# A 31-tap depthwise convolution: tap blocks made on chip, and four taps moved from TensorE to ScalarE and GpSimd

## The chip, the cores and the metric

The kernel runs on one core of a Trainium2 chip. The metric is device time in microseconds (us) of one execution. Before the change three runs gave 1594.94, 1595.30 and 1595.79 us, with a median of 1595.3 us.

## The reference

One inference step of a two-layer encoder trunk, for 256 frames of a new stream and 16 frames each of 8 running streams: 384 tokens of 1024 features, all in fp32. Layer 1 has a SwiGLU feed-forward block, a Conformer convolution module and a second feed-forward block. Layer 2 has the same with attention in the middle. The convolution module is what is changed:

```python
def _conv_module(h, prev, pw1_w, pw1_b, dw_w, dw_b, cln_g, cln_b, pw2_w, pw2_b):
    u = h @ pw1_w + pw1_b
    u = u[..., :D_MODEL] * jax.nn.sigmoid(u[..., D_MODEL:])
    u_full = jnp.concatenate([prev, u], axis=1)          # prev: the 30 rows before
    z = lax.conv_general_dilated(u_full, dw_w[:, None, :], window_strides=(1,),
        padding='VALID', feature_group_count=D_MODEL) + dw_b   # 31 taps, each channel alone
    z = jax.nn.silu(_layer_norm(z, cln_g, cln_b))
    return z @ pw2_w + pw2_b, u_full[:, -(CONV_K - 1):]
```

So each output of the depthwise convolution is a sum of 31 products of a channel's value at 31 neighbouring frames with 31 weights of that channel.

## The kernel before, in words

Activations lie with the features on the 128 partitions: 8 tiles (`KT`) of 128 features by 384 tokens, 256 of them (part 0) of the new stream, 128 (part 1) of the eight running ones. A dense product is made of units: a 128x1024 block of weights lands in `raw`, ScalarE rounds it to fp32r in `wH` (line 788), VectorE takes the rest into `wL` (line 1047), and TensorE makes three 384-column products for each 128x128 block (lines 1494 and 1502). The ring holds four units: unit n+4 is refilled when TensorE is through with unit n, and each refill has its fixed place in ScalarE's and VectorE's programs. Every engine has one instruction stream written out by hand, which it runs in order; they meet at semaphores. There is no scheduler.

The convolution stage runs over the tiles d = 0 to 7. For tile d, TensorE makes the two pointwise products (units 2d and 2d+1 of the stage, banks 2j and 2j+1 with j = d % 2). ScalarE takes the sigmoid of the second (line 897), VectorE multiplies and writes the gated row `uF[:, d]` (lines 1340 and 1341). SP and ScalarE then issue 16 DMAs, eight each (`shifted_rows`, line 402), which copy the 128 rows of `uF[:, d]` into four tiles `u4`, shifted by 0 to 3 frames in the four groups of 32 partitions. With these, one TensorE product of a 128x32 block does four taps for 32 channels: the block holds a diagonal of weights for each tap. `taps(d)` on TensorE (line 1671) goes over 7 groups (`QUADS`) of four taps, 4 groups of channels and the two parts, 56 matmuls, and comes three tiles late: `taps(d-3)` stands after the pointwise products of tile d, and `taps(5)`, `taps(6)`, `taps(7)` follow the last of them. The blocks with the diagonals (128x896 for a tile) are made on the host and loaded by DMA (line 412). The three taps that are left are done by VectorE on `uF` (`rest_taps`, lines 1317 to 1322), which starts from the subtracted mean `cS` for tiles 1 to 7, and `conv_out_tile` (line 1330) adds them to TensorE's bank, into `z[:, d]`.

`cS` is the mean of tile 0 of `z`: VectorE makes `z[:, 0]` in its round for tile 3, TensorE multiplies it by ones between the two units of tile 4 (`shift`, line 1572), and ScalarE copies the result (line 797) at the head of its round for tile 4. GpSimd has little to do in the stage: the residual `xa` (lines 694 and 696), the subtraction from tile 0 (line 633), the 16 copies of the last 30 frames for the output (lines 723 and 724), and the running sums of the tiles and of their squares (`zs`, line 646, and `sqs`, line 655) up to tile 6. The squares come from ScalarE (line 809). Two last products with ones (lines 1576 to 1587) give mean and variance for the layer norm, which ends the stage.

ScalarE's round for tile d before the change:

```python
            for d in range(KT):
                refill(n + RING, 2 * j)              # the first unit of tile d + 2
                a.activation(sg[:, j, :], ...)       # sigmoid of tile d
                refill(n + RING + 1, 2 * j + 1)      # the second unit of tile d + 2
                shifted_rows(act, d, 2)              # 8 DMA issues, which wait for u_done
                shifted_rows(act, d, 3)
                if d > 3:
                    square(1, d - 4)
```

Of the kernel before, what the change touches and what calls it, by code (L numbers as in the profile page):

```python
# [21 lines left out]
P = 128  # L22
# [13 lines left out]
QUADS = CK // 4  # L36
REST = CK - 4 * QUADS
# [59 lines left out]
_par("dw_rest", REST * KT)  # L97
# [48 lines left out]
def build_program(nc, W, ADA0, ADA, par_d, con_d, x_d, c_d, conv_d, cw_d, kt_d, v_d, lf_d, wf_d,  # L146
                  y_o, kT_o, v_o, lf_o, conv_o, nc_d):
    with ExitStack() as ctx:
# [31 lines left out]
        taps4 = at("taps4", [P, 2, QUADS + 1, P], hid + 4 * KT * UW)  # L180
        o4 = hid + 4 * KT * UW + 8 * (QUADS + 1) * P
# [5 lines left out]
        assert o4 + 56 * UW <= hid + 2 * FT * T * 4  # L187
# [72 lines left out]
        tapsT = at("tapsT", [P, QUADS, P], tmp.manual_sbuf_range[0])  # L260
# [48 lines left out]
        taps_in = [sem(f"taps_in{i}") for i in range(3)]  # L309
        u4_in = [sem(f"u4_in{i}") for i in range(4)]  # L310
        silu_done, rest_done = sem("silu_done"), sem("rest_done")
# [15 lines left out]
        TAP_PLACE = ((0, 0), (1, 0), (0, 1), (1, 1), (0, 2), (2, 0), (0, 3), (1, 2))  # L327
# [77 lines left out]
        def tap_tile(d):  # L405

            s = TAP_PLACE[d][0]
            return tapsT[:] if s == 2 else taps4[:, s, 0:QUADS]

        def load_taps(queue, d):  # L410

            queue.dma_start(tap_tile(d), cw_d[d].rearrange("p (q c) -> p q c", q=QUADS))\
                .then_inc(taps_in[TAP_PLACE[d][0]], 16)

# [4 lines left out]
        def _(sp):  # L419
# [99 lines left out]
            load_taps(sp, 1)  # L519
            load_taps(sp, KT - 3)  # L520
# [17 lines left out]
            sp.wait_ge(cv_mm, KT - 2)  # L538
            piece(B_CONV_GAP[2], 0)
# [85 lines left out]
        def _(pool):  # L625
# [87 lines left out]
            residual(1)  # L713
            center(1, 0)
            for k in range(1, KT - 1):
                add_tile(1, k)
                add_square(1, k)
                if k == 4:
                    pool.wait_ge(u_done, 2 + KT)
                    pool.wait_ge(cv_mm, k + 1)  # L720
                    for d in range(KT):
                        to = conv_st[:, d] if d < KT - 1 else conv_end[:]
                        g.tensor_copy(to[:, 0:HIST], uF[:, d, SEQ:SEQ + HIST])
                        op = g.tensor_copy(
                            to[:, HIST:].rearrange("p (b t) -> p b t", b=DB),
                            uF[:, d, HIST + SEQ:UROW].rearrange("p (b t) -> p b t", b=DB)[:, :, DS:DS + HIST])
                    op.then_inc(convst_ok, 1)
# [52 lines left out]
        def _(act):  # L780
# [108 lines left out]

            for d in range(KT):  # L890
                j, n = d % 2, U_PW1 + 2 * d
                if d == 4:
                    shift(1)
                refill(n + RING, 2 * j)
                act.wait_ge(w_used, n + 2)
                act.wait_ge(u_done, d + 1)
                a.activation(sg[:, j, :], bank[2 * j + 1][:, 0:T], ACT.Sigmoid,
                             bias=pcol("pw1_b", KT + d)).then_inc(sig_done, 1)
                refill(n + RING + 1, 2 * j + 1)
                act.wait_ge(u_done, 2 + d + 1)  # L900
                if d > 3:
                    act.wait_ge(cv_mm, d - 3)
                shifted_rows(act, d, 2)
                if d == KT - 1:
                    act.wait_ge(cv_mm, KT - 3)
                    load_taps(act, KT - 2)
# [127 lines left out]
        def _(dve):  # L1034
# [267 lines left out]

            def rest_taps(d):
# [3 lines left out]
                shift = (cS[:, 0:SEQ], cS[:, SEQ:T].rearrange("p (b t) -> p b t", b=DB))  # L1307
                if d > 0:
                    dve.wait_ge(cs_done, 2)
                if d > 1:  # L1310
                    dve.wait_ge(z_ready, 2 + KT + d - 1)
                for q in range(REST):
                    w = pcol("dw_rest", KT * q + d)
                    for part in range(2):
                        src = window(uF[:, d], 4 * QUADS + q)[part]
                        if q == 0 and d == 0:
                            op = v.tensor_scalar(acc[part], src, w, None, ALU.mult)
                        elif q == 0:
                            op = v.scalar_tensor_tensor(acc[part], src, w, shift[part], ALU.mult, ALU.subtract)
# [13 lines left out]
            for d in range(KT):  # L1333
# [12 lines left out]
                if d > 2:  # L1346
                    conv_out_tile(d - 3)
            rest_taps(KT - 3)
            conv_out_tile(KT - 3)
            rest_taps(KT - 2)  # L1350
# [130 lines left out]
        def _(pe):  # L1481
# [174 lines left out]
            def taps(d):  # L1656

                out = bank[4 + d % 2]
                place, use = TAP_PLACE[d]
                weights = tap_tile(d)  # L1660
                pe.wait_ge(taps_in[place], 16 * use + 16)
# [258 lines left out]
def _tap_blocks(w):  # L1920
# [3 lines left out]
    cw = np.zeros((KT, 4, 32, QUADS, 4, 32), np.float32)  # L1924
    c = np.arange(32)
    cw[:, :, c, :, :, c] = taps.reshape(QUADS, 4, KT, 4, 32).transpose(4, 2, 1, 0, 3)
    return cw.reshape(KT, P, QUADS * P)
# [81 lines left out]
```

## Time and profile before

| | us |
|---|---|
| median of three runs | 1595.3 |
| the profiled execution | 1594.26 |
| its span | 1592.5 |
| PE busy in the span | 1559.2 (98%) |
| DVE busy | 796.0 (50%) |
| ACT busy | 594.4 (37%) |
| POOL busy | 263.7 (17%) |
| the convolution stage, from its first separate unit to the last product with ones | 345.93 to about 441 |

In the chain of waits, "issue" is time in which an engine waited for nothing that the profile shows. An engine name with a q, as ACTq, is its queue of DMA issues.

### The profile page before, as it was taken

The page shows a single profiled execution, that of the slowest core. Times are in us where ns is not written, and L with a number is a line of the kernel's source. Part 1 is how long each engine was busy: PE and PEld are TensorE (multiplying, and loading weights), DVE is VectorE, ACT ScalarE, POOL GpSimd, SP SyncE. Part 2 cuts the span into 40 slices and gives each one's busy share as a digit, 9 for nine tenths or more (in the row PEclk, how much of TensorE's full clock was granted, in tenths as well). Part 3 has the DMA queues.
Part 4 walks back from the last instruction along what each step waited for, and adds up shares of the span by engine and source line. Part 5 has one row for each costly group of instructions (what it writes and reads, how often), then busy time and mean ns, then how long its engine had stood idle before and what let it go on. Part 6 is the DMA issues. An engine that isn't in the chain of part 4 may idle for free.

```text
span 1592.5 us, 31097 instructions
## 1 busy us (share of the span) xinstructions
PE 1559.2 (98%) x12550; PEld 1493.5 (94%) x12550; DVE 796.0 (50%) x1246; ACT 594.4 (37%) x897; POOL 263.7 (17%) x307
## 2 busy tenths in 40 slices
PE   6999999999999999999999999999998999999998
PEld 5999999998789999999988999999997899999997
DVE  3433344475588434344654433344567684444443
ACT  3433333342155333333343433333346554333332
POOL 1100002250335000012340000002252052000111
PEclk9999999999999999999999999999999999999999
DMA  9545466579983455556417554566556824333441
GB/s 373 182 163 184 158 216 222 183 238 276 275 336 102 172 195 179 191 199 225 163 54 252 188 183 158 182 226 236 187 220 242 290 94 132 132 121 118 143 142 44
DMA packets 86748, 301.66 MB, mean 189 GB/s; under 512 B 10784, under 2 KB 14160, under 8 KB 85328
## 3 DMA queue, kind: packets, MB, share of 16 engines
q1 hardware_dynamic: 83440, 294.55, 54.1%
q10 hardware_dynamic: 3216, 5.80, 1.4%
q8 instruction: 68, 1.11, 0.3%
q14 instruction: 24, 0.20, 0.0%
HBM read 283.31 MB, written 6.32 MB: 182 GB/s over the span
## 4 chain that ended last, share of the span: by engine, by line
PE 87%; DVE 5%; issue 3%; ACT 2%; DMA 1%; POOL 1%; SPq 1%; ACTq 0%; DVEq 0%; POOLq 0%
PE bank L1494 71%; PE bank L1502 8%; PE bank L1531 3%; DVE wL L1047 1%; PE bank L1731 1%; DMA land<-ADA 1%; ACT wH L788 1%; PE bank L1671 1%; PE bank L1825 1%; PE bank L1796 1%; DVE hL L1185 1%; DVE z L1082 0%; PE bank L1767 0%; SPq L495 0%; DVE z L1089 0%
## 5 line engine op out<-in xcount | busy, mean ns | idle before, releaser
L788 ACT ACTIVATE wH<-raw 128x1024 fp32r<-128x1024 f32 x328 | 345.6, 1057 | 507.3 <-PE bank L1494 469.9
L1494 PE MATMUL bank<-hH,wH 128*128 128x384 f32 x1496 | 502.9, 336 | 0.8 <-DVE wL L1047 0.8
L1047 DVE TENSOR_TENSOR wL<-raw,wH 128x1024 fp32r<-128x1024 f32 x328 | 415.8, 1294 | 174.3 <-ACT wH L788 171.4
L1494 PE MATMUL bank<-hH,wL 128*128 128x384 f32 x1496 | 500.0, 334 | 0.0
L1494 PE MATMUL bank<-hL,wH 128*128 128x384 f32 x1496 | 499.8, 334 | 0.0
L1494 PEld LDWEIGHTS bank<-hH,wH 128*128 128x128 f32 x1496 | 280.8, 188 | 5.1 <-DVE wL L1047 2.4
L1494 PEld LDWEIGHTS bank<-hL,wH 128*128 128x128 f32 x1496 | 280.9, 188 | 0.4
L1494 PEld LDWEIGHTS bank<-hH,wL 128*128 128x128 f32 x1496 | 280.8, 188 | 0.0
L1230 DVE TENSOR_TENSOR tmp<-sg,bank 128x384 f32<-128x384 f32 x88 | 48.8, 554 | 431.8 <-PE bank L1494 414.2
L1494 PE MATMUL bank<-hidH,wH 128*128 128x384 f32 x704 | 237.0, 337 | 0.0
L1494 PE MATMUL bank<-hidH,wL 128*128 128x384 f32 x704 | 235.3, 334 | 0.0
L1494 PE MATMUL bank<-hidL,wH 128*128 128x384 f32 x704 | 235.2, 334 | 0.0
L633 POOL TENSOR_TENSOR z<-z,cS 128x384 f32<-128x384 f32 x7 | 8.1, 1162 | 890.0 <-ACT cS L797 890.0
L854 ACT ACTIVATE sg<-bank 128x384 f32<-128x384 f32 x88 | 43.2, 491 | 254.5 <-PE bank L1494 235.6
L1494 PEld LDWEIGHTS bank<-hidH,wH 128*128 128x128 f32 x704 | 132.2, 188 | 1.7 <-DVE z L1219 0.6
L1494 PEld LDWEIGHTS bank<-hidL,wH 128*128 128x128 f32 x704 | 132.2, 188 | 0.5
L1494 PEld LDWEIGHTS bank<-hidH,wL 128*128 128x128 f32 x704 | 132.2, 188 | 0.0
L1502 PE MATMUL bank<-hH,wH 128*128 128x384 f32 x232 | 79.4, 342 | 4.4 <-DVE hL L1185 2.6
L1502 PE MATMUL bank<-hH,wL 128*128 128x384 f32 x232 | 77.7, 335 | 0.0
L1502 PE MATMUL bank<-hL,wH 128*128 128x384 f32 x232 | 77.6, 335 | 0.1
L655 POOL TENSOR_TENSOR sqs<-sqs,sqb 128x384 f32<-128x384 f32 x34 | 50.8, 1495 | 147.5 <-ACT sqb L809 147.5
L809 ACT ACTIVATE sqb<-z 128x384 f32<-128x384 f32 x56 | 28.6, 516 | 65.1 <-DVE z L1219 26.3
(224 smaller groups left out, 1578.1 us busy)
## 6 DMA issues: line engine op xcount, KB each, us to landing
raw<-W SPq DMA_DIRECT2D x328, 512.0 KB, 3.7
araw<-ADA SPq DMA_DIRECT2D x52, 512.0 KB, 5.7
gapZ<-ADA SPq DMA_DIRECT2D x36, 512.0 KB, 4.9
land<-ADA SPq DMA_DIRECT2D x16, 512.0 KB, 15.3
gapE<-ADA SPq DMA_DIRECT2D x16, 512.0 KB, 4.2
KTb<-kt_d SPq DMA_DIRECT2D x8, 1024.0 KB, 7.0
Vb<-v_d SPq DMA_DIRECT2D x8, 1024.0 KB, 5.2
gapH<-ADA SPq DMA_DIRECT2D x12, 512.0 KB, 4.5
```

The lines of the kernel that those rows point to most:

```text
L655: g.tensor_tensor(sqs[:], sqs[:], sqb[:, k % 2], ALU.add).then_inc(sqs_done, 1)
L788: a.activation(wH[:, slot, :], raw[:, slot, :], ACT.Copy).then_inc(w_hi, 1)
L809: a.activation(sqb[:, k % 2], z[:, k, :], ACT.Square).then_inc(sq_done, 1)
L854: a.activation(sg[:, j, :], bank[2 * j][:, 0:T], ACT.Silu).then_inc(sg_done, 1)
L1047: v.tensor_tensor(wL[:, slot, :], raw[:, slot, :], wH[:, slot, :].bitcast(F32), ALU.subtract)\
L1185: v.tensor_tensor(lo[:, ks, :], src[:, ks, :], hi[:, ks, :].bitcast(F32), ALU.subtract)\
L1230: v.tensor_tensor(tmp[:, j, :], sg[:, j, :], bank[2 * j + 1][:, 0:T], ALU.mult)\
L1494: op = mm(out, tile_w(w, slot, k), m[:, k0 + k, :], start=start and k == 0 and q == 0, stop=stop and k == nk - 1 and q == 2)
L1502: op = mm(bank[j][:, 0:T], tile_w(w, j, k), m[:, k, :], start=k == 0 and q == 0, stop=k == KT - 1 and q == 2)
L1531: op = mm(out[32 * j:32 * j + 32, 0:cols], cact[:, k, :], tile[:, cols * j:cols * j + cols], start=start, stop=stop)
L1671: op = mm(acc, weights[:, q, rows], src, start=q == 0, stop=q == QUADS - 1)
L1731: op = mm(bank[4 * half + t][:, :], h[:, k, tok], w[:, j, 512 * kk:512 * kk + 512], start=k == 0 and q == 0, stop=k == KT - 1 and q == 2)
```

## The change

- TensorE does 6 groups of four taps and not 7: 48 matmuls for a tile and not 56.
- The four taps 24 to 27 (`INNER`) go to ScalarE and GpSimd. ScalarE multiplies the windows of `uF[:, d]` by a column of weights: the first product goes to `z[:, d]`, the next three into the two halves of `tmp` in turn, each in two parts. GpSimd adds these three to `z[:, d]`. For tiles 1 to 7 GpSimd then subtracts `cS` from it. ScalarE's products for tile d stand at the end of its round for tile d. Before the first one it waits for the residual `xa`, which reads the old `z`.
- VectorE's three taps (28 to 30) now start from `z[:, d]`; they wait for `taps_moved` (for tile 0 for `pool_taps`) where before they waited for `cS`.
- The blocks with the diagonals aren't loaded any more. One small load brings the weights and a 32x32 identity for all tiles (128x224), and VectorE multiplies them out to 128x768 for each tile (`make_taps`).
- GpSimd's order is other: its copies of the last frames now stand behind the three sums of tile 7.

```diff
-QUADS = CK // 4
-REST = CK - 4 * QUADS
+QUADS = 6
+INNER = 4
+REST = CK - 4 * QUADS - INNER
...
-                if 2 < d < KT - 1:
-                    sp.wait_ge(cv_mm, d - 2)
-                    load_taps(sp, d - 1 if d < KT - 2 else KT - 1)
-
-            load_taps(sp, 0)
-            load_taps(sp, 1)
-            load_taps(sp, KT - 3)
+
+            sp.dma_start(tapw[:], cw_d).then_inc(taps_in, 16)
...
             sp.wait_ge(cv_mm, KT - 2)
+            sp.wait_ge(pool_taps, (INNER - 1) * KT)
             piece(B_CONV_GAP[2], 0)
...
+            def add_taps(d):
+
+                for q in range(1, INNER):
+                    pool.wait_ge(act_taps, INNER * d + q + 1)
+                    if q > 1:
+                        pool.wait_ge(pool_taps, (INNER - 1) * d + q - 1)
+                    g.tensor_tensor(z[:, d, :], z[:, d, :], tmp[:, (q - 1) % 2, :], ALU.add).then_inc(pool_taps, 1)
+
+            def shift_taps(d):
+
+                pool.wait_ge(cs_done, 2)
+                pool.wait_ge(pool_taps, (INNER - 1) * (d + 1))
+                g.tensor_tensor(z[:, d, :], z[:, d, :], cS[:], ALU.subtract).then_inc(taps_moved, 1)
+
+            for d in range(4):
+                add_taps(d)
+            for d in range(1, 4):
+                shift_taps(d)
             center(1, 0)
-            for k in range(1, KT - 1):
+            for d in range(4, KT):
+                add_taps(d)
+                shift_taps(d)
+                if d == KT - 1:
+                    pool.wait_ge(cv_mm, 5)
+                    for t in range(KT):
...
+                add_tile(1, d - 3)
+                add_square(1, d - 3)
+            for k in range(5, KT - 1):
                 add_tile(1, k)
                 add_square(1, k)
...
+            def inner_taps(d):
+
+                if d == 0:
+                    act.wait_ge(xa_done, 2 * KT)
+                for q in range(INNER):
+                    if d > 0 and q in (1, 2):
+                        act.wait_ge(pool_taps, (INNER - 1) * d + 1 - q)
+                    elif q == 3:
+                        act.wait_ge(pool_taps, (INNER - 1) * d + 1)
+                    to = z[:, d] if q == 0 else tmp[:, (q - 1) % 2]
+                    parts = (to[:, 0:SEQ], to[:, SEQ:T].rearrange("p (b t) -> p b t", b=DB))
+                    for part in range(2):
+                        op = a.activation(parts[part], window(uF[:, d], 4 * QUADS + q)[part], ACT.Identity,
+                                          scale=pcol("dw_rest", KT * q + d))
+                    op.then_inc(act_taps, 1)
...
                 shifted_rows(act, d, 3)
                 if d > 3:
                     square(1, d - 4)
+                inner_taps(d)
...
+            def make_taps(d):
+
+                if d < 2:
+                    dve.wait_ge(taps_in, 16)
+                else:
+                    dve.wait_ge(cv_mm, d - 1)
+                n = 4 * QUADS
+                v.tensor_tensor(taps4[:, d % 2, 0:QUADS * P].rearrange("p (n c) -> p n c", n=n),
+                                tapw[:, n * d:n * d + n].unsqueeze(2).to_broadcast([P, n, 32]),
+                                tapw[:, n * KT:n * KT + 32].unsqueeze(1).to_broadcast([P, n, 32]), ALU.mult)\
+                    .then_inc(taps_made, 1)
+
+            make_taps(0)
+            make_taps(1)
...
                 if d > 0:
-                    dve.wait_ge(cs_done, 2)
+                    dve.wait_ge(taps_moved, d)
+                else:
+                    dve.wait_ge(pool_taps, INNER - 1)
...
                     conv_out_tile(d - 3)
+                    make_taps(d - 1)
...
-                pe.wait_ge(taps_in[place], 16 * use + 16)
+                pe.wait_ge(taps_made, d + 1)
```

ScalarE before, its round for tile 1: `wH` is a refill, `sg` the sigmoid, the DMA rows are the shifted copies.

```order
L788 ACTIVATE wH<-raw 128x1024 [waits w_in2,w_used]
L897 ACTIVATE sg<-bank,par 128x384 [waits u_done,w_used]
L788 ACTIVATE wH<-raw 128x1024 [waits w_in3,w_used]
L402 DMA u_64<-uF 32x652 [waits u_done]
L402 DMA u_64<-uF 32x652 x7
```

And after, the same round:

```order
L802 ACTIVATE wH<-raw 128x1024 [waits w_in2,w_used]
L927 ACTIVATE sg<-bank,par 128x384 [waits u_done,w_used]
L802 ACTIVATE wH<-raw 128x1024 [waits w_in3,w_used]
L403 DMA u_64<-uF 32x652 [waits u_done]
L403 DMA u_64<-uF 32x652 x7
L916 ACTIVATE z<-uF,par 128x256
L916 ACTIVATE z<-uF,par 128x128
L916 ACTIVATE tmp<-uF,par 128x256 [waits pool_taps]
L916 ACTIVATE tmp<-uF,par 128x128
```

Behind these stand two more such pairs into `tmp`, and then the refill of the next round. So eight activations now stand between the shifted copies of one tile and the refills of the next.

GpSimd before, from the sums of tile 4 to the end of the stage (14 more copies stand where the dots are); `zs` is the running sum of tiles, `sqs` that of squares, `conv_st` the output copies.

```order
L723 COPY conv_st<-uF 128x30 [waits cv_mm,u_done]
L724 COPY conv_st<-uF 128x240
...
L646 TENSOR_TENSOR zs<-zs,z 128x384 [waits ys_done,z_ready]
L655 TENSOR_TENSOR sqs<-sqs,sqb 128x384 [waits sqs_done,sq_done]
L646 TENSOR_TENSOR zs<-zs,z 128x384 [waits ys_done,z_ready]
L655 TENSOR_TENSOR sqs<-sqs,sqb 128x384 [waits sqs_done,sq_done]
L633 TENSOR_TENSOR z<-z,cS 128x384 [waits cs_done]
```

And after, from the sums of tile 7's products:

```order
L712 TENSOR_TENSOR z<-z,tmp 128x384 [waits act_taps]
L712 TENSOR_TENSOR z<-z,tmp 128x384 [waits pool_taps,act_taps] x2
L718 TENSOR_TENSOR z<-z,cS 128x384 [waits pool_taps,cs_done]
L732 COPY conv_st<-uF 128x30 [waits cv_mm]
L733 COPY conv_st<-uF 128x240
...
L637 TENSOR_TENSOR zs<-zs,z 128x384 [waits ys_done,z_ready]
L646 TENSOR_TENSOR sqs<-sqs,sqb 128x384 [waits sqs_done,sq_done]
```

The last two rows come three times, for tiles 4, 5 and 6. The copies and three pairs of sums now stand behind the last product of tile 7; before, the copies and two pairs stood behind the fifth round of taps and nothing of tile 7.

VectorE after, its round for tile 4 (`mS` is the accumulator of tile 1, `uF` the gated row of tile 4):

```order
L1362 SCALAR_TENSOR_TENSOR mS<-uF,par,z 128x256 [waits taps_moved]
L1362 SCALAR_TENSOR_TENSOR mS<-uF,par,z 128x128
...
L1383 SCALAR_TENSOR_TENSOR uF<-bank,par,sg 128x256 [waits sig_done]
L1384 SCALAR_TENSOR_TENSOR uF<-bank,par,sg 128x8x16
```

Before:

```order
L1319 SCALAR_TENSOR_TENSOR mS<-uF,par,cS 128x256 [waits cs_done]
L1319 SCALAR_TENSOR_TENSOR mS<-uF,par,cS 128x128
...
L1340 SCALAR_TENSOR_TENSOR uF<-bank,par,sg 128x256 [waits sig_done]
L1341 SCALAR_TENSOR_TENSOR uF<-bank,par,sg 128x8x16
```

The head of the round now waits for GpSimd's `taps_moved`, behind four tiles of ScalarE's products, where it waited for the copy of the mean.

## Rows read from the trace of the kernel before

**Rows 1.** Windows of the stage: length, busy time of each engine, PE clock, DMA.

```profile
383.00:419.00 36.00, 36.00 (x417) 32.11 (x419) 13.36 (x29) 8.69 (x12) 3.96 (x4) 1.00 0.97 274
```

**Rows 2.** TensorE in order of time: start, length, idle time before in brackets.

```profile
345.93 0.41 PE L1494 MATMUL bank<-hH,wH 128*128 128x384 f32 x1 [0.82 <-DVE wL L1047]
...
362.75 4.76 PE L1671 MATMUL bank<-u,taps 128*32 128x256 f32 x112
...
371.71 0.81 PE L1572 MATMUL bank<-z,con 128*128 128x384 f32 x2
```

**Rows 3.** ScalarE in order of time, rounds 1 to 5.

```profile
350.09 1.06 ACT L788 ACTIVATE wH<-raw 128x1024 fp32r<-128x1024 f32 x1 [5.50 <-issue]
351.05 0.56 ACT L897 ACTIVATE sg<-bank,par 128x384 f32<-128x384 f32 x1
351.52 1.05 ACT L788 ACTIVATE wH<-raw 128x1024 fp32r<-128x1024 f32 x1
352.43 5.04 ACTq L402 DMA_DIRECT2D u<-uF  x8
...
359.91 6.04 ACTq L402 DMA_DIRECT2D u<-uF  x8
...
374.90 0.49 ACT L797 ACTIVATE cS<-bank 128x384 f32<-128x384 f32 x1 [6.06 <-issue]
...
378.94 6.51 ACTq L402 DMA_DIRECT2D u<-uF  x8
385.50 0.53 ACT L809 ACTIVATE sqb<-z 128x384 f32<-128x384 f32 x1 [7.26 <-issue]
...
392.19 5.60 ACTq L402 DMA_DIRECT2D u<-uF  x8
```

**Rows 4.** ScalarE's groups over the whole span, shapes apart: busy, mean ns.

```profile
L836 ACT ACTIVATE h<-z,Bm,Am 128x256 f32<-128x256 f32 x40 | 23.4, 592 | 28.8 <-DVE Bm L1161 13.8 <-DMA z<-x_d 10.7 <-DVE z L1089 4.3
L841 ACT ACTIVATE hH<-h 128x384 fp32r<-128x384 f32 x34 | 17.9, 526 | 22.9 <-POOL h L685 22.3 <-DVE h L1148 0.2
L920 ACT ACTIVATE h<-z,par 128x384 f32<-128x384 f32 x8 | 5.7, 708 | 2.9 <-DVE z L1089 2.0 <-PE bank L1531 0.3
L883 ACT ACTIVATE conR<-con 128x128 fp32r<-128x128 f32 x1 | 0.3, 292 | 0.0
```

**Rows 5.** GpSimd in order of time.

```profile
352.52 2.46 POOL L696 TENSOR_SCALAR xa<-z,gA,bA 128x128 f32<-128x128 f32 x1
375.47 1.32 POOL L633 TENSOR_TENSOR z<-z,cS 128x384 f32<-128x384 f32 x1 [20.50 <-ACT cS L797]
...
429.52 0.27 POOL L723 COPY conv_st<-uF 128x30 f32<-128x30 f32 x1
...
434.36 1.18 POOL L646 TENSOR_TENSOR zs<-zs,z 128x384 f32<-128x384 f32 x1
...
437.65 1.04 POOL L655 TENSOR_TENSOR sqs<-sqs,sqb 128x384 f32<-128x384 f32 x1
```

**Rows 6.** GpSimd's two groups over the whole span: busy, mean ns.

```profile
L646 POOL TENSOR_TENSOR zs<-zs,z 128x384 f32<-128x384 f32 x27 | 35.8, 1328 | 36.4 <-DVE z L1219 36.4
L633 POOL TENSOR_TENSOR z<-z,cS 128x384 f32<-128x384 f32 x7 | 8.1, 1162 | 890.0 <-ACT cS L797 890.0
```

**Rows 7.** VectorE in order of time.

```profile
344.42 2.51 DVE L1047 TENSOR_TENSOR wL<-raw,wH 128x1024 fp32r<-128x1024 f32 x2
...
382.84 0.74 DVE L1319 SCALAR_TENSOR_TENSOR rstd<-uF,par,cS 128x256 f32<-128x256 f32 x2
383.50 1.40 DVE L1322 SCALAR_TENSOR_TENSOR rstd<-uF,par,rstd 128x256 f32<-128x256 f32 x4
391.41 0.48 DVE L1340 SCALAR_TENSOR_TENSOR uF<-bank,par,sg 128x256 f32<-128x256 f32 x1 [6.52 <-ACT sg L897]
```

**Rows 8.** Windows at the start and end of the span, columns as in Rows 1.

```profile
0.00:10.00 10.00, 1.93 (x64) 1.72 (x64) 0.45 (x4) 1.70 (x2) 0.20 (x4) 1.00 0.83 291
1584.00:1592.00 8.00, 3.65 (x12) 1.84 (x10) 4.29 (x9) 5.05 (x8) 0.00 (x0) 0.92 0.50 197
```

More of the change, by code:

```diff
@@ L308, in build_program @@
             "hist_ok", "sig_done", "u_done", "cv_mm", "convst_ok"))
-        taps_in = [sem(f"taps_in{i}") for i in range(3)]
+        taps_in, taps_made = sem("taps_in"), sem("taps_made")
         u4_in = [sem(f"u4_in{i}") for i in range(4)]
-        silu_done, rest_done = sem("silu_done"), sem("rest_done")
+        silu_done, rest_done, act_taps, pool_taps, taps_moved = (sem(n) for n in (
+            "silu_done", "rest_done", "act_taps", "pool_taps", "taps_moved"))
         kf_done, vs_done, f_mm, lf_chain, ncum_done, lfo_done = (sem(n) for n in (
@@ L405, in tap_tile @@
         def tap_tile(d):
[L407 to L413, printed above, removed]
+            return taps4[:, d % 2, 0:QUADS * P].rearrange("p (q c) -> p q c", q=QUADS)
         block = ctx.enter_context(nc.Block())
@@ L713, in _ @@
             residual(1)
-            center(1, 0)
-            for k in range(1, KT - 1):
+            def add_taps(d):
[12 more added lines that the diff above has]
+                shift_taps(d)
+            center(1, 0)
+            for d in range(4, KT):
[4 more added lines that the diff above has]
+                    for t in range(KT):
+                        to = conv_st[:, t] if t < KT - 1 else conv_end[:]
+                        g.tensor_copy(to[:, 0:HIST], uF[:, t, SEQ:SEQ + HIST])
+                        op = g.tensor_copy(
+                            to[:, HIST:].rearrange("p (b t) -> p b t", b=DB),
+                            uF[:, t, HIST + SEQ:UROW].rearrange("p (b t) -> p b t", b=DB)[:, :, DS:DS + HIST])
+                    op.then_inc(convst_ok, 1)
+                add_tile(1, d - 3)
+                add_square(1, d - 3)
+            for k in range(5, KT - 1):
                 add_tile(1, k)
                 add_square(1, k)
[L718 to L727, printed above, removed]
             sums(2)
@@ L1312, in rest_taps @@
                 for q in range(REST):
-                    w = pcol("dw_rest", KT * q + d)
+                    w = pcol("dw_rest", KT * (INNER + q) + d)
                     for part in range(2):
[L1315 to L1319, printed above, removed]
+                        src = window(uF[:, d], 4 * QUADS + INNER + q)[part]
+                        if q == 0:
+                            op = v.scalar_tensor_tensor(acc[part], src, w, inner[part], ALU.mult, ALU.add)
                         else:
@@ L1923, in _tap_blocks @@
     taps[:] = w[:4 * QUADS]
[L1924 to L1927, printed above, removed]
+    of = taps.reshape(QUADS, 4, KT, 4, 32).transpose(1, 4, 2, 0, 3).reshape(P, KT * 4 * QUADS)
+    return np.concatenate([of, np.tile(np.eye(32, dtype=np.float32), (4, 1))], 1)
 def _constants():
@@ L1963 @@
     put("dw_b", _cols(i["dw_b"]))
-    put("dw_rest", np.concatenate([_cols(i["dw_w"][0][4 * QUADS + q]) for q in range(REST)], 1))
+    put("dw_rest", np.concatenate([_cols(i["dw_w"][0][4 * QUADS + q]) for q in range(INNER + REST)], 1))
     par[0:H, PAR["b_f"][0]] = i["b_f"]
```

18 lines of the change are left out of this document (7 added, 11 removed).

## The prediction

> **What bounds the kernel now.** I read the busy times first: TensorE is busy for 1559.2 of 1592.5 us, so at first sight all that is taken from it is gained. Then the windows of the convolution stage: from 383 to 419 us TensorE has no gap at all, at a granted clock of 1.00, while ScalarE seems busy for 8.69 of 36 us [rows 1]. That share misleads, since DMA issues are not in it. In order of time ScalarE's refill at 350.09 had been idle 5.50 us for "issue": the eight shifted copies of tile 0 held the engine [rows 3]. A round of ScalarE is a refill, the sigmoid, a refill (starts 350.09, 351.05, 351.52, 352.43: 2.34 us together) and eight issues: 5.04, 6.04, 6.51 and 5.60 us for eight in four rounds, so 23.19/32 = 0.725 us each, 5.8 us a round [rows 3]. That is 8.1 us. A round of TensorE is two units, (362.75 - 345.93)/4 = 4.2 us each, and 4.7 us of taps from tile 3 on [rows 2]: 8.4 us at first, 13.1 us later. So ScalarE is full in the first rounds and has about 4.5 us to spare in the later ones. The stage ends in GpSimd's sums: the last one is over at 437.65 + 1.04 = 438.69 us [rows 5], and the products with ones wait for it.
>
> **What is taken away.** TensorE: one of seven groups, 4.7/7 = 0.67 us a tile, 5.4 us in all [rows 2]. SP issues fewer loads and ScalarE one less; both wait or have room there, and I count that at nothing. If nothing else came late the stage would be 5.4 us shorter at most.
>
> **VectorE's blocks.** 768 columns with two operands from SBUF. The nearest row is the 1024-column subtraction, 2.51 us for two [rows 7], so 0.95 us; by columns alone from the same row also 0.94. Two are made ahead of the first gated row, which delays the first unit by about 1.1 us (TensorE already waits 0.82 there [rows 2]); this vanishes in what follows. The other six lie where VectorE idles, as the 6.52 us before 391.41 [rows 7]. I take nothing, bounds 0 and 2.
>
> **ScalarE's products.** Each tap is an activation of 256 and one of 128 columns with its scale read from a column. The 256-column one with scale and bias from columns takes 592 ns; from 256 to 384 columns that form rises to 708, so 128 columns take about 0.48 [rows 4]. Back to back each starts 0.09 us before the last has ended (the refill of 1.06 us at 350.09 and the next start at 351.05 [rows 3]). So 0.50 + 0.39 = 0.9 us a tap. The bounds: as cheap as a plain copy (292 ns at 128 columns, 526 at 384, so 0.41 at 256 [rows 4]), less the overlaps, 0.52; and 1.07 without overlap. I take 0.9, since the form with a scale column is the nearest. Four taps are 3.6 us, and the fourth must wait until GpSimd has added the second (its half of `tmp` must be free): a sum of 1.08 us (four in the 4.33 us from 434.36 to 438.69 [rows 5]) and 0.06 us to each side against the 0.9 of the third product, so 0.3 us. A tile costs ScalarE 3.9 us, eight cost 31. In the later rounds nearly all the room is used; in the first ones none is there.
>
> **The walk.** The products of tile 0 wait for the residual, over at 352.52 + 2.46 = 355.0 [rows 5]; they are done at 358.9. Only then does ScalarE refill the first unit of tile 3, which was done at 350.09 before. Sigmoid 360.4, gated row 361.1, VectorE's half of the refill 1.2 us later: TensorE starts tile 3 at 362.4 and not at 354.3, after a wait of about 7 us. Rounds 1, 2 and 3 of ScalarE are 2.34 + 5.8 + 3.9 = 12.0 us: 395.0. In between TensorE meets its second wait. The product of the mean stands between the two units of tile 4 and needs `z[:, 0]`, which VectorE makes in round 3, behind the gated row and the refills. The sigmoid of tile 3 ends at 358.9 + 24.1 + 1.4 = 384.4; gated row 0.7, refills 2.4 (half of 2.51 each, less overlap), `z` 0.6: 388.1. TensorE is there at 362.4 + 8.4 + 4.0 + 4.2 = 379.0 and waits 9 us. Before, it came to that point at 371.71 without a wait [rows 2].
>
> Round 4: the copy of the mean 0.4, refills and sigmoid 2.34: 397.7. Now the shifted copies need the gated row of tile 4, which in VectorE stands behind its three taps of tile 1, which now wait for GpSimd: third sum of tile 3 at 396.1, subtraction of the mean 1.16 (its mean time [rows 6]) 397.3, taps 0.66 + 1.40 [rows 7] 399.4, gated row 400.1. A wait of 2.4 us. Then issues, a square of 0.5 and products: 410.3. Rounds 5, 6 and 7 are 2.34 + 5.8 + 0.5 + 3.9 = 12.5 us: 447.9. GpSimd then adds the last product (449.1), subtracts the mean (450.2), makes the 16 copies, which took 434.36 - 429.52 = 4.84 us [rows 5] (455.1), and adds three tiles and three squares, six sums of 1.08 (461.6). Against 438.69 that is 22.9 us later. TensorE, from 388.1 on, comes to about 453 with its taps, inside this. What follows in the stage and behind it is as before. The profiled execution took 1594.26 us: 1594.3 + 22.9 = 1617.2; the median of runs was 1.0 us above it. I say 1617.
>
> **A rule on the sums.** GpSimd's sum of two 384-column tiles took 1.04 to 1.18 us at the stage's end [rows 5], but 1328 ns in the mean of all 27 [rows 6]. The Trainium skill (SBUF — State Buffer, "SBUF: two separate sides") says that VectorE and GpSimd share a pair of ports which one locks for a whole instruction, also against a VectorE operation with two SBUF inputs, while ScalarE has its own. The trace agrees in direction: the residual's piece at 352.52 took 2.46 us beside VectorE's 1024-column subtraction. In a sentence that the sum does not need: by this rule the new sums, which meet VectorE's refills and blocks more often, would come at 1.3 and not at 1.08.
>
> **Rivals.**
> 1. *The issues do not hold ScalarE* (the other side). If products could run beside the issues, its round would be 2.34 + 3.9 + 0.5 = 6.7 us, under TensorE's 12.4 everywhere; TensorE's 5.4 us would be gained, less 1.1 at the first unit: 1590. It decides from where ScalarE's round is under TensorE's. Against it: the refill at 350.09 that had been idle 5.50 us for the issues, when units had long been free [rows 3]. 4%.
> 2. *It is all off the path* or gain and loss are even: 1594. Nothing in the rows makes them equal. 2%.
> 3. *Cheap products and issues.* 0.52 us a tap takes 0.38 x 32 = 12 us from ScalarE's sum, and issues as in round 1 (0.63) take 56 x 0.095 = 5 us. Then TensorE's own series is next, so not all of it counts: from about 1604 to 1611, say 1608. For it: the windows are read in plain order. Against it: the scale from a column. 20%.
> 4. *GpSimd under contention.* Sums of 1.33 us [rows 6] add 0.25 us at eight waits, the last product and six sums, 3.8 us, and full-length products (1.07) 5.4: 1626. 12%.
> 5. *The clock.* In the first 10 us of the span TensorE is busy for 1.93 us and the granted clock is 1.00; in the last window, 3.65 us busy of 8, it is 0.92 [rows 8]. If it fell to 1.2 GHz after the waits of 7, 9 and 8 us, a unit would take 8.4 us for 4.2 and the two products at the end the same: up to 4 us for each wait, of which those of the middle hide behind ScalarE: 1621. 7%. The Trainium skill (TensorE: Matmul & The Clock Gate, "What's actually happening") says that an idle array is set to 1.2 GHz until work returns; by that rule this rival would be certain, and the row of the start speaks against it.
>
> **Chances and range.** The forecast, 1612 to 1622, has 55%. Adding both lower ends gives about 1604 and both upper ends with contention about 1630; 8 in 10 lie in 1605 to 1628. A measurement of this kernel tells 0.2% (3.2 us) from no change. Faster is rival 1, 4%; same is rival 2, 2%; the rest is slower, 94%.
>
> **What would show it.** In the profile after: ScalarE without idle time other than "issue" from 355 to about 448; eight activations of `uF` in 3.9 us a tile; TensorE waiting some 7 us for `wL` ahead of tile 3 and some 9 us for `z` ahead of the mean of tile 4, with its taps 4.0 us long; VectorE waiting for GpSimd at the head of round 4; the copies behind the last products, and the sums over at about 461. It is wrong if TensorE has no gap between 345 and 430, if a tap costs under 0.6 us, or if the stage ends under 450.

## The result, and the profile after

The changed kernel takes 1615.7 us in the median of four runs (1614.75 to 1620.26), the one before 1595.2 us beside it. The ratio is 1.0128, with an interval of 1.0112 to 1.0144: slower by 20.5 us. The forecast was 1617 us with a range of 1605 to 1628, so sign and size came out. The profiled execution took 1614.82 us with a span of 1612.7, against 1594.26 and 1592.5: 20.6 us more. Not all of it came the way I had put it, as the rest shows.

The busy times on the page of the changed kernel (us, share of the span, instructions of each engine):

```profile
PE 1560.4 (97%) x12422; PEld 1494.7 (93%) x12422; DVE 803.0 (50%) x1254; ACT 617.2 (38%) x961; POOL 298.8 (19%) x338
```

TensorE has fewer products and is yet busy for 1.2 us longer: a first sign that some of them ran slowly. Its waits between 335 and 475 us (what waited, for whom, sum, times, longest):

```profile
PE bank L1621 <- POOL zs L637: 9.1, 1, 9.1
PE bank L1539 <- DVE wL L1075: 7.6, 2, 5.9
PE bank L1617 <- DVE z L1373: 4.1, 1, 4.1
```

These are the three gaps that were forecast: for the refill of tile 3 (5.9 of the 7.6 us; the other 1.7 lie ahead of the first unit), for `z` ahead of the mean of tile 4, and for GpSimd's sums at the end. TensorE in order of time, to set beside [rows 2]:

```profile
347.03 0.41 PE L1539 MATMUL bank<-hH,wH 128*128 128x384 f32 x1 [1.70 <-DVE wL L1075]
...
361.50 0.66 PE L1539 MATMUL bank<-hH,wH 128*128 128x384 f32 x1 [5.91 <-DVE wL L1075]
361.96 0.52 PE L1539 MATMUL bank<-hL,wH 128*128 128x384 f32 x1
362.28 0.52 PE L1539 MATMUL bank<-hH,wL 128*128 128x384 f32 x1
...
371.96 0.33 PE L1539 MATMUL bank<-hL,wH 128*128 128x384 f32 x1
372.13 0.34 PE L1539 MATMUL bank<-hH,wL 128*128 128x384 f32 x1
...
384.96 1.65 PE L1617 MATMUL bank<-z,con 128*128 128x384 f32 x2 [4.07 <-DVE z L1373]
```

After the wait of 5.91 us the products follow each other every 0.32 us; ten us later every 0.17. The same product costs about twice as much right behind a wait. The windows say why (columns as in [rows 1]):

```profile
363.00:371.00 8.00, 8.00 (x38) 8.00 (x37) 0.71 (x3) 5.17 (x11) 3.03 (x3) 0.77 0.96 259
379.00:388.00 9.00, 4.93 (x18) 4.01 (x18) 4.40 (x6) 3.88 (x8) 2.09 (x3) 0.77 0.65 197
400.00:420.00 20.00, 20.00 (x224) 18.10 (x226) 10.54 (x21) 10.14 (x23) 7.54 (x8) 1.00 0.92 283
...
455.00:465.00 10.00, 8.01 (x104) 5.10 (x108) 3.17 (x8) 3.88 (x5) 2.80 (x3) 0.63 0.80 322
```

The granted clock is a mean between two levels, 2.4 and 1.2 GHz. It is 1.00 where TensorE had no gap (400 to 420), 0.77 around the two waits in the middle and 0.63 behind the 9.1 us at the end. This fits what the Trainium skill (TensorE: Matmul & The Clock Gate, "What's actually happening") says of an idle array, whose clock is let down to 1.2 GHz. The start of the span [rows 8], by which I gave that rule 7 in 100, was no evidence against it, as two rows of the kernel before show:

```profile
7.85 1.93 PE L1531 MATMUL bank<-land,cact 128*32 128x64 f32 x64 [7.85 <-DMA land<-ADA]
...
23.51 2.23 PE L1531 MATMUL bank<-land,cact 128*32 128x64 f32 x128
```

Records of the same kind of product took 1.93/64 = 0.030 us each in the first ten us and 2.23/128 = 0.017 at 23.5 us, though the granted clock reads 1.00 in both stretches. So a reading of 1.00 at the start does not show fast products. That the clock was low there is likely, but no record shows it.

ScalarE in order of time, beside [rows 3]:

```profile
354.62 0.80 ACT L916 ACTIVATE z<-uF,par 128x256 f32<-128x256 f32 x2 [9.80 <-POOL xa L687]
355.33 1.48 ACT L916 ACTIVATE tmp<-uF,par 128x256 f32<-128x256 f32 x4
357.23 0.81 ACT L916 ACTIVATE tmp<-uF,par 128x256 f32<-128x256 f32 x2 [0.42 <-POOL z L712]
357.94 1.04 ACT L802 ACTIVATE wH<-raw 128x1024 fp32r<-128x1024 f32 x1
...
360.25 5.11 ACTq L403 DMA_DIRECT2D u<-uF  x8
...
421.29 5.91 ACTq L403 DMA_DIRECT2D u<-uF  x8
```

A tap starts 0.71 us after the one before it (354.62, 355.33), and a tile's four, with the wait of 0.42 us for GpSimd's sum, take 357.94 - 354.62 = 3.32 us, not 3.9. The two shapes apart (busy, mean ns of one):

```profile
L916 ACT ACTIVATE tmp<-uF,par 128x256 f32<-128x256 f32 x24 | 12.0, 499 | 3.7 <-POOL z L712 3.7
L916 ACT ACTIVATE tmp<-uF,par 128x128 f32<-128x128 f32 x24 | 9.4, 393 | 0.0
```

VectorE in order of time, beside [rows 7]:

```profile
384.29 0.61 DVE L1373 SCALAR_TENSOR_TENSOR z<-bank,par,rstd 128x384 f32<-128x384 f32 x1
384.82 0.94 DVE L1338 TENSOR_TENSOR taps<-tapw 128x768 f32<-128x768 f32 x1
393.19 2.24 DVE L1362 SCALAR_TENSOR_TENSOR mS<-uF,par,z 128x256 f32<-128x256 f32 x2 [7.42 <-POOL z L718]
395.35 2.15 DVE L1365 SCALAR_TENSOR_TENSOR mS<-uF,par,mS 128x256 f32<-128x256 f32 x4
397.41 0.47 DVE L1383 SCALAR_TENSOR_TENSOR uF<-bank,par,sg 128x256 f32<-128x256 f32 x1
```

A block takes 0.94 us alone, as worked out. The head of round 4 waits for GpSimd, and the gated row of tile 4 comes at 397.4 to 398.15. GpSimd's end of the stage, beside [rows 5]:

```profile
442.02 3.87 POOL L712 TENSOR_TENSOR z<-z,tmp 128x384 f32<-128x384 f32 x3 [0.38 <-ACT tmp L916]
446.04 1.27 POOL L718 TENSOR_TENSOR z<-z,cS 128x384 f32<-128x384 f32 x1
447.26 0.27 POOL L732 COPY conv_st<-uF 128x30 f32<-128x30 f32 x1
...
452.05 0.98 POOL L637 TENSOR_TENSOR zs<-zs,z 128x384 f32<-128x384 f32 x1
...
456.80 1.00 POOL L646 TENSOR_TENSOR sqs<-sqs,sqb 128x384 f32<-128x384 f32 x1
```

The last sum is over at 457.80 against 438.69: 19.1 of the 20.6 us stand there. The chain that ended last goes on from it (start, us, what). The profile shows each product of these fp32 kinds as two records: the 56 of `taps(d)` before are x112 in [rows 2], so x2 is one product. First before, then after:

```profile
437.83 0.88 PE bank L1576 x2
...
440.95 2.76 PE bank L1531 x96
443.71 1.64 issue
```

```profile
393.69 3.90 PE bank L1715 x96
397.60 8.54 PE bank L1539 x48
...
456.99 1.62 PE bank L1621 x2
...
461.17 1.28 PE bank L1632 x2
462.44 5.38 PE bank L1576 x192
467.82 12.22 PE bank L1547 x69
```

The same four products (eight records) took 3.1 us before and 5.45 after, 2.3 us more; they are at 1.2 GHz behind the wait. The next piece then gives back 1.85 us: its 192 records were held up for 1.64 us in the middle before, and now run through in 5.38. So the next piece's end is at 467.82 against 448.18, 19.6 us later, and little more is added up to the span's end (20.2).

### The profile page after: what moved, and what is told of

Its sections match the earlier page's. It is cut to its first block, busy times and chain, and to the rows that moved or that the text cites. A ratio compares the mean times of both kernels' runs of the same rounds, so it can differ in the third digit from the quotient of the medians.

```text
span 1612.7 us, 30960 instructions
## 1 busy us (share of the span) xinstructions
PE 1560.4 (97%) x12422; PEld 1494.7 (93%) x12422; DVE 803.0 (50%) x1254; ACT 617.2 (38%) x961; POOL 298.8 (19%) x338
## 4 chain that ended last, share of the span: by engine, by line
PE 88%; DVE 4%; ACT 2%; POOL 2%; issue 1%; DMA 1%; ACTq 1%; SPq 1%; DVEq 0%; POOLq 0%
PE bank L1539 71%; PE bank L1547 7%; PE bank L1576 4%; DMA land<-ADA 1%; PE bank L1775 1%; ACTq L403 1%; ACT wH L802 1%; PE bank L1715 1%; DVE wL L1075 1%; DVE hL L1213 1%; PE bank L1869 1%; PE bank L1840 1%; DVE z L1117 0%; POOL xa L685 0%; DVE z L1110 0%
## 5 line engine op out<-in xcount | busy, mean ns | idle before, releaser
L1539 PEld LDWEIGHTS bank<-hH,wH 128*128 128x128 f32 x1496 | 282.3, 189 | 12.3 <-issue 9.3
```

Of the source, the lines that this page charges most:

```text
L1539: op = mm(out, tile_w(w, slot, k), m[:, k0 + k, :], start=start and k == 0 and q == 0, stop=stop and k == nk - 1 and q == 2)
```

## The experiments

All are compared with the kernel before on the same chip, and their edits are shown against the changed kernel where nothing else is said.

**Without the products and their sums.** ScalarE's products and GpSimd's sums go, VectorE begins from `cS` as before, and GpSimd's copies and sums stand again as in the kernel before; the blocks and the six groups stay. Taps 24 to 27 are then missing from the result.

```diff
-            for d in range(4):
-                add_taps(d)
-            for d in range(1, 4):
-                shift_taps(d)
...
-                inner_taps(d)
...
-                    dve.wait_ge(taps_moved, d)
-                else:
-                    dve.wait_ge(pool_taps, INNER - 1)
+                    dve.wait_ge(cs_done, 2)
```

> The changed kernel without ScalarE's products and GpSimd's sums: taps 24 to 27 are left out of the result, TensorE does six groups, VectorE makes the blocks and does its three taps as before. Theory A (the products hold ScalarE and with it the refills, the gated rows and the last sums; the rest of the change is worth what TensorE saves): TensorE starts the stage about 1.1 us late behind the two blocks, then saves 0.67 us in each of 8 tiles, so about 4 us faster than before: 1591, from 1589.5 to 1592.5, and no wait of TensorE over 2 us between 347 and 430 us. Rival B (the blocks on VectorE delay the gated rows or the taps): 1596 or more, with TensorE waiting for the blocks.

Measured: ratio 0.9997 (0.9988 to 1.0006), no change, where I had expected 1591. Two things follow. The whole loss comes with the products, the sums and the order of GpSimd's work. And TensorE's saving is worth nothing by itself. TensorE's longest wait in that run:

```profile
PE bank L1581 <- POOL zs L636: 5.1, 1, 5.1
```

The 5.4 us that six groups save lie there as a wait of 5.1 us for GpSimd's sums, which end at 438.23 + 1.00 = 439.23, half a us later than before. Behind that wait the four products with ones took 4.33 us (438.42 to 442.75) in place of 3.12: slow products take 1.2 us of the saving. TensorE was almost without a gap before and still not alone in setting the end.

**The blocks alone.** All seven groups on TensorE, their blocks made by VectorE; the computation is whole.

```diff
-QUADS = 6
-INNER = 4
+QUADS = CK // 4
+INNER = 0
```

GpSimd's order is that of the kernel before again.

> The kernel before with the blocks for seven groups made by VectorE (896 columns) in place of the loads, and nothing on ScalarE and GpSimd; nothing is left out. Theory A: the two blocks ahead of the first gated row cost about 1.2 us once, the others lie in VectorE's idle time; fewer DMA issues are worth nothing: 1596.5, from 1595.3 to 1598. Rival B: each block delays the path by its own length, about 1.1 us a tile: 1602 or more.

Measured: ratio 1.0011 (1.0002 to 1.0020), 1.8 us slower, near the upper one of my bounds, 0 and 2. Making the blocks on chip brings no time. In its profile TensorE waits 2.0 us at the first unit and 2.1 us for the sums, and the four products behind that take 4.69 us (439.72 to 444.41) in place of 3.12.

**The products without the sums.** ScalarE makes all products, nobody adds them, and GpSimd's copies and sums stand as in the kernel before. The result is again without taps 24 to 27.

```diff
-                    if d > 0 and q in (1, 2):
-                        act.wait_ge(pool_taps, (INNER - 1) * d + 1 - q)
-                    elif q == 3:
-                        act.wait_ge(pool_taps, (INNER - 1) * d + 1)
-                    to = z[:, d] if q == 0 else tmp[:, (q - 1) % 2]
+                    if 4 * d + q > 1:
+                        act.wait_ge(act_taps, 4 * d + q - 1)
+                    to = tmp[:, q % 2]
```

> The changed kernel with ScalarE's products made but not used: GpSimd does no sums of them and no subtractions, VectorE starts from the mean as before, so taps 24 to 27 are missing in the result. Theory A (ScalarE's occupancy is the loss up to the last round, GpSimd's part only its sums and their place behind the last tile): both waits of TensorE, 5.9 us ahead of tile 3 and some 4 us ahead of the mean of tile 4, stay, the end comes 4 to 7 us earlier than in the changed kernel: 1610, from 1608 to 1612. Rival B (GpSimd's sums are the loss): 1600 or less, near the kernel without products, 1595.6.

Measured: ratio 1.0094 (1.0079 to 1.0110), 15.1 us slower. TensorE's waits:

```profile
PE bank L1515 <- DVE wL L1051: 7.1, 2, 5.4
PE bank L1597 <- POOL zs L637: 5.6, 1, 5.6
PE bank L1593 <- DVE z L1349: 3.7, 1, 3.7
```

All three gaps stay. So 15 of 20 us come with ScalarE's work alone, and GpSimd's sums of products, its subtractions and their order add 5. The parts do not simply add up: GpSimd's copies lie between ScalarE's last squares and the last sums in this run too (443.70 to 448.53), so a part of the 15 us is theirs.

**Four of ScalarE's eight shifted copies issued by SP.**

```diff
-                for t in range(2):
+                for t in range(3):
...
-                shifted_rows(act, d, 2)
```

> The changed kernel with four of ScalarE's eight shifted copies of each tile issued by SP. ScalarE's round is 2.6 us shorter. Theory A (ScalarE's occupancy sets the pace up to the mean of tile 4, later ScalarE and TensorE are level): the wait ahead of tile 3 stays (it comes from the residual), the one ahead of the mean of tile 4 goes, and the last products are over 5 to 8 us earlier: 1608, from 1605 to 1611. Rival B (SP's twelve issues a tile, or the copies' landing, are late in turn): 1613 or more. Rival C (GpSimd's sums, not ScalarE, are the pace): no change, 1615 to 1616.

Measured: ratio 1.0065 (1.0049 to 1.0080) where the changed kernel has 1.0128 (1.0112 to 1.0144): 9.6 to 10 us of the loss go, and nothing of the computation was changed. ScalarE's rounds 1 and 2 take 8.1 and 8.4 us (refills at 357.81, 365.95 and 374.30), where they took 10.8 and 11.1 in the changed kernel (357.94, 368.75, 379.82). TensorE's two longest waits:

```profile
PE bank L1538 <- DVE wL L1074: 7.6, 2, 5.9
PE bank L1620 <- POOL zs L637: 5.3, 1, 5.3
```

The first gap stays: the products of tile 0 wait for the residual, whoever issues. The gap at the mean is gone. This is the test of the step on which all rested, that issuing transfers holds ScalarE: rival 1 is out.

**Sixteen products without use ahead of the mean's sums**, so that TensorE is at work while it would wait.

```diff
+            keep_clock(16)
             stats(1, B_CONV_GAP, bank[3])
```

> The changed kernel with 16 products without use on TensorE (into a bank that is free there) between its last taps and the mean, in the time in which it waits for GpSimd's sums. Theory A (the clock that fell during the wait costs time on the path): the four products at the end take about 3.2 us and not 5.5, and the 24 small ones behind them are faster: 2 to 3 us faster than the changed kernel, 1613. Rival B (the products at the end at half the clock are hidden, or the added ones run over the wait): 1615.5 to 1618.

Measured: ratio 1.0116 (1.0100 to 1.0131), which overlaps with the changed kernel's. The chain in its profile:

```profile
457.90 1.41 PE bank L1621 x2
...
461.80 0.65 PE bank L1632 x2
462.44 5.38 PE bank L1576 x192
```

The four products take 4.54 us and not 5.45, 0.9 us less, because the last ones are fast again; the sums happened to end 0.9 us later in that execution, so the next piece starts at the same 462.44. In the window of 450 to 465 us the granted clock was still 0.89, as TensorE waited 2.1 us behind the useless products. So about 1 us could be had back here in the profile; the 2 to 3 us were not reached, and the times of the two kernels are not far enough apart to show the 1 us.

**GpSimd's copies behind its last sums**, in the changed kernel and in the one before (here the edit of the latter).

```diff
-                if k == 4:
-                    pool.wait_ge(u_done, 2 + KT)
-                    pool.wait_ge(cv_mm, k + 1)
-                    for d in range(KT):
...
+            pool.wait_ge(u_done, 2 + KT)
+            pool.wait_ge(cv_mm, 5)
+            for d in range(KT):
```

> The changed kernel with GpSimd's 16 copies moved behind the last running sums of the stage. Theory A (the copies, 4.8 us from 447.26 to 452.05, lie on the path between the last products and the last sums): the sums are over 4.8 us earlier, though the last tile of z, ready at 452.0, then ends the stage: between 3 and 5 us faster than the changed kernel, 1611.5. Rival B (something else, as ScalarE's last squares, takes the place): within 1 us of the changed kernel, 1615.

> The kernel before with the same move of the copies, nothing else. TensorE's last taps end at 436.9 and the mean waits 0.8 us for GpSimd, so theory A gives at most 1 us: 1594.5, from 1593.5 to 1596. Rival B (the copies, now late, hold up what SP loads behind them): 1597 or more.

Measured: 1.0100 (1.0084 to 1.0115) from the changed kernel, 3.8 us less than the changed kernel's 1615.7; 0.9998 (0.9989 to 1.0007) from the kernel before. The copies of 4.8 us are on the path after the change and were not before it: there, VectorE's taps of tile 7 and its last `z` (until 438.59) were as late as the sums (438.69).

**The same, with the products and sums left out**, as in the first experiment.

> Six groups on TensorE, blocks by VectorE, taps 24 to 27 left out of the result, copies moved behind the sums. Without the move this took 1595.6, with a wait of 5.1 us of TensorE for GpSimd's sums. Theory A (TensorE's saving had gone into that wait, and the copies made it): 3 to 4.5 us faster than before, 1592. Rival B (the wait comes from ScalarE's last DMA issues and squares, which the move leaves): 1594.5 to 1596.

Measured: 0.9992 (0.9983 to 1.0001), 1.3 us and not 3 or more; the interval still holds no change. The wait for the sums is gone and TensorE waits 2.0 us for VectorE. VectorE in order of time:

```profile
426.11 2.24 DVE L1321 SCALAR_TENSOR_TENSOR rstd<-uF,par,cS 128x256 f32<-128x256 f32 x2
428.28 3.63 DVE L1324 SCALAR_TENSOR_TENSOR rstd<-uF,par,rstd 128x256 f32<-128x256 f32 x4
```

The four instructions of two taps that take 1.40 us alone [rows 7] take 3.63 beside GpSimd's sums. With the copies ahead of the sums they had taken 2.29, and VectorE's last `z` of the stage was over at 435.78; now it is over at 437.58, against an end of the sums of 439.23 there. So of the 4.8 us freed on GpSimd the stage can see 1.7 at most; against the run with the copies ahead (0.9997) it saw 0.8 us, within the noise of both. The Trainium skill (SBUF — State Buffer, "SBUF: two separate sides") states that a VectorE operation with two inputs in SBUF and a GpSimd operation shut each other out; this trace agrees in direction, with 3.63 us for 1.40.

**All seven remaining taps on VectorE**, six groups on TensorE, no products on ScalarE, copies late; whole computation. This would be the way to keep TensorE's saving without ScalarE.

```diff
-INNER = 4
+INNER = 0
...
-            make_taps(0)
-            make_taps(1)
...
+                if d > 3:
+                    rest_taps(d - 2)
+            rest_taps(KT - 2)
```

> The whole computation with six groups on TensorE and all seven other taps on VectorE, none on ScalarE and GpSimd; VectorE's rounds do the gated row first and the taps of tile d-2 last, the first two blocks are made behind the first refills, and GpSimd's copies stand behind the sums. Four more taps are 2.8 us of VectorE a tile, where it idled 5 to 6.5 us. Theory A (the loss was ScalarE's, and VectorE has the room): 4 us faster than before, 1592, from 1590 to 1595. Rival B (VectorE's taps delay its refills, gated rows or the last tile): 1597 or more.

Measured: 1.0018 (1.0009 to 1.0027), 2.9 us slower. TensorE's longest wait:

```profile
PE bank L1677 <- DVE taps L1297: 4.7, 1, 4.7
```

The block of tile 7 is made behind the fourteen instructions of taps of tile 6 (two for each of seven taps), and VectorE becomes the bound at the end. Behind that wait the clock is down again: a set of TensorE's products for the four groups of channels of tile 7 takes 0.42 us from 433.23 on, and 0.21 us in the run with the products without use.

**A mixed form of the kernel before**: loaded blocks, six groups for tiles 0 to 4 with seven taps on VectorE, seven groups and three taps for tiles 5 to 7, copies late; whole computation. The edit is against the kernel before.

```diff
+        def rests(d):
+            return REST + 4 if d < 5 else REST
...
-                    for q in range(QUADS):
+                    quads = QUADS - 1 if d < 5 else QUADS
+                    for q in range(quads):
```

> The kernel before with six groups on TensorE for tiles 0 to 4 alone, whose four taps go to VectorE (2.7 us a tile, in rounds in which it idled 6.5 us); tiles 5 to 7 stay at seven groups, blocks are loaded as before, GpSimd's copies stand behind the sums. The whole computation. Theory A (TensorE's saving counts where the engine that takes the taps has room, and the last three tiles have none): 5 x 0.67 = 3.3 us less TensorE in the rounds, 2 to 3.5 us faster than before, 1593.3. Rival B (the last tile's shifted copies, ScalarE's last squares or the port that VectorE and GpSimd share take the place): within 1 us of before.

Measured: 0.9996 (0.9987 to 1.0005), no difference from before. TensorE's waits, the two longest:

```profile
PE bank L1537 <- issue: 2.0, 1, 2.0
PE bank L1678 <- DMA taps<-cw_d: 1.5, 1, 1.5
```

The first products with ones behind the sums start 1.1 us earlier than before (436.77 against 437.83), and the next stage 1.0 us earlier (447.16 against 448.18). The wait of 1.5 us for a load of blocks ahead of them had taken the rest. That 1.0 us is not seen in the span of this execution (1593.2 against 1592.5) nor in the medians; no run shows where it goes.

**The three repairs together**: SP issues four copies, GpSimd copies late, and each tile's products a round later, behind the shifted copies of the next; whole computation.

```diff
+                if d > 0:
+                    inner_taps(d - 1)
...
-                inner_taps(d)
+            inner_taps(KT - 1)
```

> The changed kernel with three moves at once: SP issues four of ScalarE's eight copies a tile (9.6 us faster alone), GpSimd's copies stand behind the sums (3.8 us alone), and ScalarE makes the products of a tile one round later, behind the refills, so that the wait for the residual doesn't hold the refill of tile 3 (5.9 us of TensorE's wait). The whole computation. Theory A (the three are separate parts of the loss): TensorE has no wait over 2 us between 347 and 430, 1598, from 1595 to 1601, still not under the kernel before. Rival B (ScalarE's total work is the loss wherever it stands): 1603 or more.

Measured: 1.0068 (1.0050 to 1.0087), no better than SP's issues alone. The first gap is gone (1.7 us as in the run without products), but other waits have come. TensorE's longest, then VectorE at the head of round 4:

```profile
PE bank L1715 <- DMA u_low<-uF: 4.5, 1, 4.5
```

```profile
389.13 2.24 DVE L1362 SCALAR_TENSOR_TENSOR mS<-uF,par,z 128x256 f32<-128x256 f32 x2 [12.81 <-POOL z L718]
```

VectorE waits 12.81 us for GpSimd's subtraction. The mean was there at 379.2, but in GpSimd's order the subtraction stands behind the sums of tile 3's products, and these were over at 388.1 only, since ScalarE now makes those products a round later. The gated row of tile 4 and its shifted copies stand behind that, and ScalarE's issues for it start only at 394.14. SP's twelve start there too, and the weight load behind them holds a refill of ScalarE until 413.4. Of the versions run, none is faster than the kernel before.

## Why the prediction was right, point by point

1. *What bounds the stage.* Right: ScalarE is held by the issues. Moving 4 of 8 gives 10 us, the products without the sums cost 15. The share of busy time (10.1 of 20 us from 400 to 420) would still say that ScalarE idles half the time.
2. *TensorE saves 0.67 us a tile.* Right in size: 48 products (96 records) in 4.04 and 3.90 us where 56 took 4.7, and the wait of 5.1 us in the run without ScalarE's products. "If nothing else came late" was the right proviso: it is worth nothing alone. What is late next is the end of GpSimd's sums, 439.2 against 438.7.
3. *Blocks.* 0.94 each, the first unit 1.1 us later (347.03 against 345.93). The whole edit costs 1.8 us; to take nothing of it was the lower one of my bounds, and it came out near the upper.
4. *A tap 0.9 us.* Mis-sized: 0.71. I had taken the form with scale and bias from columns (592 ns at 256 columns); the measured ones are 499 and 393 ns, at 256 columns 93 ns under that nearest row and between it and the copy's 0.41. Over 32 taps that is 0.19 x 32 = 6 us less. The other half of rival 3, cheap issues, came only in part: the six full groups of eight issues from 345.72 to 421.29 took 5.11, 5.11, 5.37, 5.30, 5.58 and 5.91, so 32.38/48 = 0.675 each, against 0.725.
5. *The wait for GpSimd's sum.* 0.42 us for 0.3.
6. *The walk.* Products of tile 0 from 354.6, as said (355.0). TensorE at tile 3: 361.50 for 362.4, a wait of 5.9 for 7. `z` of tile 0 at 384.9 for 388.1, the wait 4.1 for 9, for two reasons: ScalarE's rounds are 10.9 us and not 12.0 ((390.62 - 357.94)/3), and TensorE came to it later, at 380.9 for 379.0, since its units were slow. Head of round 4: the wait is there; the gated row is over at 398.15 for 400.1. The products there were over 4.3 us earlier than forecast (390.7 for 395.0), but VectorE's taps took 2.24 + 2.15 us beside GpSimd's subtractions where I had 0.66 + 1.40.
7. *Rounds 5 to 7.* From the end of tile 4's products (407.37) to that of tile 7's (444.17) 36.8 us, 12.3 a round for 12.5. But the reason given for it is half right. I had put ScalarE alone on the path and TensorE inside. The chain goes over TensorE from 384.96 to 432.67 without a gap: a unit pair of 8.54 and taps of 3.9 to 4.0 are 12.5 us a round too. Both are level: the sigmoid at 432.19 stood 0.1 us for TensorE. So a cheaper tap than 0.71 would have brought little in these rounds.
8. *The end.* Product, subtraction, copies and six sums take 13.6 us (444.17 to 457.80) as forecast (447.9 to 461.6), with six last sums of 1.0 us, not the 1.3 of rival 4. The last product's sum and the subtraction did take 1.3 each, beside VectorE's taps (444.62 and 446.04), so rival 4 was right there, and the cheaper sums made up for it. The forecast start was 3.7 us too late, for the reasons in 4: taps and issues were both too dear.
9. *The clock.* Left out wrongly: this is the step that failed. The row of the start did not speak against it. After the waits the clock fell, each time, and products were as slow behind waits of 2.1 and 2.0 us in two other runs. Its cost on the path was 2.3 us at the end. In the middle it made TensorE's products slow as well: 16 of them took 5.26 us from 361.50 in place of 2.8, and from 384.96 the mean's product and the unit behind it took 7.7 us in place of 4.8. The first of these only made the wait at the mean shorter. The second is hidden up to some 0.2 us, because ScalarE's stream has no other idle time than its issues and GpSimd's sums from 398.18 to 432. Rival 5 was no rival but a part of the likely case.

The sum over the path: 19.1 us of later sums, and 2.3 for the clock, less 1.85 for a hold-up that is gone, are 19.6 at the head of the next stage, 20.2 at the span's end. Forecast were 22.9 for the sums and nothing for the clock. The hit at 1617 is owed in part to two errors of opposite sign, ScalarE's rounds too long by 3.8 us at the sums' end (taps and issues too dear) and the clock left out.

What stays open: why the clock read 1.00 in the first ten us, in which TensorE is hardly busy and its products are slow. That the slow products in the middle cost next to nothing is read from one trace; no run isolates it.

## What to carry to other kernels

An engine that issues transfers is not free while it does so: count 0.63 to 0.81 us for each issue, as measured here with 8 a round (5.04 to 6.51 us for eight), before giving it work that "fits in its idle time", or move the issues first. A gap of several us on TensorE costs more than its length where fast products follow, so look what the granted clock was behind such gaps, and at the pace of the products themselves, since the reading can be 1.00 where they are slow. And take a saving on the busiest engine as an upper bound: here three other chains (GpSimd's sums, VectorE's taps beside them, a transfer's landing) ended within 2 us of it, and each repair handed the bound to the next.

## What the hardware showed

- After TensorE had waited 5.9 and 4.1 us its products of 384 columns came every 0.32 us in place of 0.17, and behind 9.1 us a product with ones took 1.28 us in place of 0.65, with granted clocks of 0.77, 0.77 and 0.63 in the windows around. Waits of 2.1 and 2.0 us did the same in the run with the blocks alone (1.25 to 1.28 us) and in the one without products and with late copies (1.28).
- The granted clock read 1.00 in the first ten us, while records of one kind of product took 0.030 us each there and 0.017 at 23.5 us.
- Two of VectorE's taps took 3.6 us beside GpSimd's sums and 1.40 without. GpSimd's pieces of the residual took 1.98 and 2.57 us beside VectorE's blocks and refills and 0.55 later.
- ScalarE's activation of 256 columns took 499 ns with its scale from a column and 592 with scale and bias from columns; without either, some 0.41 us by the conversions of 128 and 384 columns [rows 4]. So an estimate from these rows is 0.09 us for each operand that comes from a column; at 384 columns two of them make 708 of 526.
